# Chunk attention: dividing the output by turned reciprocals of the row sums, and ScalarE's copies ahead of its exponentials

## The chip, the cores and the metric

The kernel runs on one core of a Trainium2 chip, as one launch. The metric is the device time of that launch in microseconds (us). Each core has a matrix engine (TensorE, "PE" in the profile, its weight loads "PEld"), a vector engine (VectorE, "DVE"), a scalar engine (ScalarE, "ACT"), a general engine (GpSimd, "POOL") and a queue engine for transfers (SyncE, "SP"). Each works through its own list in order and waits on semaphores that the others raise.

## The reference

A two-layer encoder trunk over 512 positions of width 1024. Layer 0 mixes with a state-space model and a gated delta rule, layer 1 with chunk attention; both then have a cross-attention into 256 memory rows and a gated feed-forward block. Only layer 1's chunk attention is touched:

```python
def chunk_attention(h, w_qkv, w_out, q_g, k_g, rel_bias):   # CHUNK = 64, 16 heads of 64
    qkv = (h @ w_qkv).reshape(bsz, seq, 3, CA_HEADS, CA_HEAD_DIM)
    q = rms_norm(qkv[:, :, 0], q_g); k = rms_norm(qkv[:, :, 1], k_g); v = qkv[:, :, 2]
    # each chunk of 64 rows sees itself and the 8 chunks before it
        s = jnp.einsum('bqhd,bkhd->bhqk', q_c, k_c) * scale + bias
        s = jnp.where((band_pos + start) >= 0, s, -1e30)
        p = jax.nn.softmax(s, axis=-1)
        o = jnp.einsum('bhqk,bkhd->bqhd', p, v_c)
    return o @ w_out
```

## The kernel before

The program is written out by hand, engine by engine; nothing schedules it. Big products are done as three products of rounded parts (`product`, L325 to L327), the parts being made by ScalarE (`w_hi`, L293) and VectorE (`w_lo`, L297).

Chunk attention comes after its projection and the turning of q and k. It works on **pairs**: pair m (0 to 7) holds heads 2m and 2m+1, called e = 0 and 1. The 512 query rows are four tiles i of 128, and tile i sees i+1 tiles of keys, so its row of scores is 128, 256, 384 or 512 wide. Within a query tile the rows stand in reversed order, which the last step undoes.

For one pair the steps are:

- `ca_scores_pe` (L1951), TensorE: eight products of scores, tiles in the order 3, 2, 0, 1. Tile 1 goes into the bank that tile 3 had, so it waits until VectorE has taken tile 3's scores of both heads.
- `sums` (L2043), VectorE: adds the bias and takes each row's maximum, eight instructions; then the negated maxima (L2047).
- `exp` (L2015), ScalarE: eight exponentials, each with its row sums, read out by a short instruction behind it.
- `rescale` (L2057, L2061), VectorE: for each head one reciprocal of four columns of row sums, then four multiplications that divide the probabilities.
- `ca_turn_p_pe` (L1963), TensorE: 20 transposes in eight groups n (key tile s = n // 2, head e = n % 2) of 4, 4, 3, 3, 2, 2, 1 and 1. They use the three PSUM banks 4 to 6 in turn, so group n waits for the copy of group n-3.
- `ca_copy`: the eight groups are copied to SBUF, n = 0, 2, 5, 7 by ScalarE (L1989), n = 1, 3, 4, 6 by VectorE (L1991).
- `ca_values_pe` (L1973), TensorE: eight products of values and turned probabilities into bank 7, 64 partitions for each head. It waits until the pair before has left bank 7 (`c_ol`).
- L2032, ScalarE, rounds the outputs from bank 7 to `c_o_hi`; `out_lo` (L2051), VectorE, makes the rest `c_o_lo` from bank 7. When the last pair's rest is there, the output projection begins (L325 to L327).

The order across pairs: TensorE does turn(m), scores(m+2), values(m). ScalarE does the exponentials of pair m+1 with the copies of pair m strewn between them, then `c_o_hi` of pair m. VectorE does `out_lo`(m-1), the copies of pair m with `rescale`(m+1, head 0) among them, `sums`(m+2), `rescale`(m+1, head 1). GpSimd masks the bias rows and SyncE loads them; both are ahead by a pair.

Of the kernel before, what the change touches and what calls it, by code (L numbers as in the profile page):

```python
# [7 lines left out]
F32 = mybir.dt.float32  # L8
# [67 lines left out]
def build_program(nc, A):  # L76
    ctx = ExitStack()
    with ctx:
# [9 lines left out]
        with nc.sbuf_tensor("params", [P, N_PAR], F32) as par:  # L88
# [23 lines left out]
                   "c_pv2": ("sv_u", LEVELS * TT),  # L112
# [1752 lines left out]
            return ps[:, bank + e, c0:c0 + (i + 1) * P]  # L1865

        c_oT = (rounded("c_o_hi", arena, KT, SEQ), rounded("c_o_lo", at_b, KT, SEQ))


        def ca_proj_pe(pe):  # L1870
# [83 lines left out]
        def ca_turn_p_pe(pe, m):  # L1954
            for n in range(8):
                s, e = n // 2, n % 2
                g = 8 * m + n
                if g >= 3:
                    pe.wait_ge(sem(COPY[(g - 3) % 8][0]), 4 * ((g - 3) // 8) + COPY[(g - 3) % 8][1])
                for i in range(s, TT):  # L1960
                    if s == 0:
                        pe.wait_ge(sem(RESCALE[i][0]), after(RESCALE[i][0], RESCALE[i][1] * (2 * m + e) + RESCALE[i][2]))
                    ins = pe.transpose(ps[:, 4 + g % 3, i * P:(i + 1) * P], p_c(m, e, i)[:, s * P:(s + 1) * P], ident)  # L1963
                ins.then_inc(sem("c_tr"), 1)

        def ca_values_pe(pe, m):
            if m > 0:
                pe.wait_ge(sem("c_ol"), m)
            for s in range(TT):
                for e in range(2):  # L1970
                    pe.wait_ge(sem(COPY[2 * s + e][0]), 4 * m + COPY[2 * s + e][1])
# [7 lines left out]
        RESCALE = [("c_pv2", 4, 4), ("c_pv2", 4, 3), ("c_pv2", 4, 2), ("c_pv2", 4, 1)]  # L1979

        def ca_copy(eng, m, n):
            s, e = n // 2, n % 2
            g = 8 * m + n
            eng.wait_ge(sem("c_tr"), g + 1)
            if m >= 1:
                eng.wait_ge(sem("c_o"), m)
            dst, src = pT_c(e, s), ps[:, 4 + g % 3, s * P:SEQ]
# [24 lines left out]
        def ca_act(a):  # L2012
            def exp(m, e, i):
                p = p_c(m, e, i)
                a.activation(p, p, ACT.Exp, bias=c_neg[:, m % 2, e, i:i + 1], accum_out=c_sum[:, m % 2, e, i:i + 1]).then_inc(sem("c_exp"), 1)  # L2015

            a.wait_ge(sem("c_max"), 1)
            for e in range(2):
                for i in CA_EXP:
                    exp(0, e, i)  # L2020
            for m in range(CH // 2):
                if m + 1 < CH // 2:
                    a.wait_ge(sem("c_max"), m + 2)
                for e in range(2):
                    for j in range(4):
                        if m + 1 < CH // 2:
                            exp(m + 1, e, CA_EXP[j])
                        n = 4 * e + j
                        if COPY[n][0] == "c_pa":
                            ca_copy(a, m, n)  # L2030
                a.wait_ge(sem("c_o"), m + 1)
                a.activation(c_oT[0][:, m, :].rearrange("p (i n) -> p i n", i=TT),  # L2032
                                  ps[:, 7, :].rearrange("p (i n) -> p i n", i=TT)[:, :, ::-1], ACT.Copy).then_inc(sem("c_oc"), 1)

        def ca_dve(v):
            def sums(m):
                v.wait_ge(sem("c_mask"), after("c_mask", 2 * m + 2))
                if m >= 2:
                    v.wait_ge(sem("c_tr"), 8 * (m - 1))
                for n, i in enumerate(CA_ROWS):  # L2040
                    v.wait_ge(sem("c_s"), 4 * m + (1, 3, 3, 4)[n])
                    for e in range(2):
                        v.tensor_tensor_reduce(out=p_c(m, e, i), in0=ca_score(i, e),  # L2043
                                                    in1=bias_ring[:, (2 * m + e) % 4, BAND_W - (i + 1) * P:BAND_W], scale=1.0, scalar=-3.0e38,
                                                    op0=ALU.add, op1=ALU.max, accum_out=c_max[:, m % 2, e, i:i + 1]).then_inc(sem("c_s2"), 1)
                v.wait_ge(sem("c_s2"), 8 * m + 8)
                v.tensor_scalar(c_neg[:, m % 2], c_max[:, m % 2], -1.0, None, ALU.mult).then_inc(sem("c_max"), 1)  # L2047

            def out_lo(m):
                v.wait_ge(sem("c_oc"), m + 1)  # L2050
                v.tensor_tensor(c_oT[1][:, m, :].rearrange("p (i n) -> p i n", i=TT),  # L2051
                                ps[:, 7, :].rearrange("p (i n) -> p i n", i=TT)[:, :, ::-1],
                                c_oT[0][:, m, :].bitcast(F32).rearrange("p (i n) -> p i n", i=TT), ALU.subtract).then_inc(sem("c_ol"), 1)

            def rescale(m, e):
                v.wait_ge(sem("c_exp"), 8 * m + 4 * e + 4)
                v.reciprocal(c_rec[:, m % 2, e], c_sum[:, m % 2, e]).then_inc(sem("c_rec"), 1)  # L2057
                v.wait_ge(sem("c_rec"), after("c_rec", 2 * m + e + 1))
                for i in (3, 2, 1, 0):
                    p = p_c(m, e, i)  # L2060
                    v.tensor_scalar(p, p, c_rec[:, m % 2, e, i:i + 1], None, ALU.mult).then_inc(sem("c_pv2"), 1)  # L2061

            sums(0)
            sums(1)
            rescale(0, 0)
            rescale(0, 1)
# [12 lines left out]
            out_lo(CH // 2 - 1)  # L2079

        def ca_pool(g):
# [397 lines left out]
```

## Time and profile before

| | |
|---|---|
| median of 3 runs | 1754.69 us (1753.34 to 1756.93) |
| the profiled execution, its own time | 1754.25 us |
| its span in the trace | 1752.5 us |
| granted TensorE clock, mean | 0.988 of full |
| TensorE busy | 1654.1 us (94%) |
| VectorE, ScalarE, GpSimd busy | 777.7, 623.0, 218.2 us |
| chunk attention, first score to the output projection's first product | about 1061.8 to 1149.8 us of the span |

The page of the profile divides the span into busy time by engine, shows a chain of waits that ended last (86% TensorE, 8% VectorE, 3% ScalarE) and lists groups of instructions. Most of the span is TensorE's big products at full rate; a change elsewhere matters only where TensorE stands waiting. "Idle before" is what an engine lost ahead of an instruction, and "issue" is time in which it waited for nothing that the profile shows.

### The profile page before, as it was taken

How to read it: one execution, taken by the hardware profiler on the slowest of the kernel's cores; microseconds unless marked ns; L12 is line 12 of the kernel's file. 1: busy time of each engine (PE TensorE's matmuls, PEld its weight loads, DVE VectorE, ACT ScalarE, POOL GpSimd, SP SyncE). 2: the span in 40 equal slices, each digit the busy share in tenths (PEclk: the TensorE clock that was granted, in tenths of full speed). 3: DMA queues.
4: the chain of work that ended last, by engine and by line, in shares of the span. 5: the costliest groups of instructions: out<-in, count | busy, mean ns of one | idle time of the engine just before them, and what ended most of it. 6: DMA issues, size and time to landing. Idle time of an engine off the chain costs nothing.

```text
span 1752.5 us, 22603 instructions
## 1 busy us (share of the span) xinstructions
PE 1654.1 (94%) x9358; PEld 1349.4 (77%) x9358; DVE 777.7 (44%) x1011; ACT 623.0 (36%) x1006; POOL 218.2 (12%) x305
## 2 busy tenths in 40 slices
PE   5989989999989999999999997899998999999999
PEld 5778788777768788888888885478776878888887
DVE  4576435544444444442235437834343444444222
ACT  6443333344433322221124335634442432222110
POOL 3843034010000211110000000000000021111000
PEclk9999999999999999999999998999999999999999
DMA  6610112134103333332222331214311233333221
GB/s 204 125 49 11 62 51 74 49 111 144 58 24 96 96 96 96 96 96 96 96 96 89 99 101 37 85 49 144 121 48 49 72 96 96 96 96 96 96 96 72
DMA packets 146802, 151.85 MB, mean 87 GB/s; under 512 B 8865, under 2 KB 109345, under 8 KB 146593
## 3 DMA queue, kind: packets, MB, share of 16 engines
q1 hardware_dynamic: 146720, 150.69, 27.9%
q8 instruction: 60, 0.98, 0.2%
q14 instruction: 22, 0.17, 0.0%
HBM read 147.53 MB, written 3.15 MB: 86 GB/s over the span
## 4 chain that ended last, share of the span: by engine, by line
PE 86%; DVE 8%; ACT 3%; issue 2%; DMA 0%; SPq 0%; POOL 0%; DVEq 0%; ACTq 0%
PE ps L325 24%; PE ps L326 24%; PE ps L327 24%; PE ps L1639 2%; PE ps L1616 2%; PE ps L1973 1%; ACT w_hi L293 1%; PE ps L955 1%; DVE sb L2043 1%; DVE sb L601 1%; DVE w_lo_ab L297 1%; PE ps L1233 1%; PE ps L417 1%; ACT sb L2015 1%; PE ps L1244 1%
## 5 line engine op out<-in xcount | busy, mean ns | idle before, releaser
L325 PE MATMUL ps<-h_hi,w_hi 128*128 128x512 f32 x864 | 338.8, 392 | 3.9 <-DVE w_lo L1787 3.9
L326 PE MATMUL ps<-h_lo,w_hi 128*128 128x512 f32 x864 | 337.6, 391 | 0.0
L297 DVE TENSOR_TENSOR w_lo<-raw,w_hi 128x2048 fp32r<-128x2048 f32 x70 | 160.4, 2292 | 395.8 <-ACT w_hi L293 395.8
L293 ACT ACTIVATE w_hi<-raw 128x2048 fp32r<-128x2048 f32 x84 | 160.7, 1914 | 433.3 <-PE ps L327 432.6
L327 PE MATMUL ps<-h_hi,w_lo 128*128 128x512 f32 x704 | 274.5, 390 | 0.0
L325 PEld LDWEIGHTS ps<-h_hi,w_hi 128*128 128x128 f32 x864 | 162.9, 189 | 38.4 <-issue 4.7
L326 PEld LDWEIGHTS ps<-h_lo,w_hi 128*128 128x128 f32 x864 | 163.1, 189 | 33.5
L1787 DVE TENSOR_TENSOR w_lo<-raw,w_hi 128x2048 fp32r<-128x2048 f32 x44 | 138.1, 3138 | 53.5 <-ACT w_hi L1769 53.5
L327 PEld LDWEIGHTS ps<-h_hi,w_lo 128*128 128x128 f32 x704 | 132.6, 188 | 27.8
L1769 ACT ACTIVATE w_hi<-raw 128x2048 fp32r<-128x2048 f32 x44 | 84.3, 1916 | 161.1 <-PE ps L327 161.1
L325 PE MATMUL ps<-w_hi,a_hi 128*128 128x512 f32 x352 | 137.3, 390 | 1.7 <-DVE up L1785 1.7
L327 PE MATMUL ps<-w_hi,a_lo 128*128 128x512 f32 x352 | 137.0, 389 | 0.0
L326 PE MATMUL ps<-w_lo,a_hi 128*128 128x512 f32 x352 | 136.9, 389 | 0.0
L1797 POOL CAST a_hi<-up 128x512 f32 x44 | 27.0, 614 | 843.1 <-DVE up L1785 843.1
L325 PE MATMUL ps<-w_hi,h_hi 128*128 128x512 f32 x320 | 124.7, 390 | 2.3 <-DVE h_lo L430 2.3
L327 PE MATMUL ps<-w_hi,h_lo 128*128 128x512 f32 x320 | 124.5, 389 | 0.0
L326 PE MATMUL ps<-w_lo,h_hi 128*128 128x512 f32 x320 | 124.5, 389 | 0.0
L1785 DVE TENSOR_TENSOR up<-up,ps 128x512 f32<-128x512 f32 x44 | 30.2, 687 | 192.7 <-PE ps L327 188.9
L1765 ACT ACTIVATE up<-up 128x512 f32<-128x512 f32 x44 | 27.8, 632 | 153.4 <-DVE up L1781 153.3
L325 PEld LDWEIGHTS ps<-w_hi,a_hi 128*128 128x128 f32 x352 | 66.1, 188 | 16.1 <-DVE up L1785 2.5
L327 PEld LDWEIGHTS ps<-w_hi,a_lo 128*128 128x128 f32 x352 | 66.1, 188 | 13.8
L326 PEld LDWEIGHTS ps<-w_lo,a_hi 128*128 128x128 f32 x352 | 66.1, 188 | 13.6
(370 smaller groups left out, 2663.0 us busy)
## 6 DMA issues: line engine op xcount, KB each, us to landing
raw<-in_f_w_gate SPq DMA_DIRECT2D x44, 512.0 KB, 4.0
raw<-in_f_w_up SPq DMA_DIRECT2D x44, 512.0 KB, 5.3
raw<-in_f_w_down SPq DMA_DIRECT2D x44, 512.0 KB, 4.1
raw<-in_xa_w_kv SPq DMA_DIRECT2D x16, 1024.0 KB, 5.0
raw<-in_c_w_qkv SPq DMA_DIRECT2D x12, 1024.0 KB, 5.0
raw<-in_ab_w_in SPq DMA_DIRECT2D x10, 1024.0 KB, 5.9
raw<-in_xa_w_q SPq DMA_DIRECT2D x8, 1024.0 KB, 5.2
raw<-in_xa_w_out SPq DMA_DIRECT2D x8, 1024.0 KB, 5.0
```

The lines of the kernel that those rows point to most:

```text
L293: a.activation(w_hi[:, n % 2, :], raw[n % 2], ACT.Copy).then_inc(sem("w_hi"), 1)
L297: v.tensor_tensor(w_lo(n)[:, n % 2, :], raw[n % 2], w_hi[:, n % 2, :].bitcast(F32), ALU.subtract).then_inc(sem("w_lo"), 1)
L325: pe.matmul(out, a[0], b[0], start=start, stop=False)
L326: pe.matmul(out, a[0], b[1], start=False, stop=False)
L327: return pe.matmul(out, a[1], b[0], start=False, stop=stop)
L1616: ins = pe.matmul(ps[:, 2 * (h % 2) + i // 2, (i % 2) * 256:(i % 2) * 256 + 256], qT[:, 2 * h + d, i * P:(i + 1) * P], xk_T[:, 2 * h + d, ...
L1639: ins = pe.matmul(ps[:, 6 + d, :], xv[:, s, h * XD + d * P:h * XD + (d + 1) * P], pT_x[h % 2][:, s, :], start=(s == 0), stop=(s == 1))
L1765: a.activation(gsil[:, s, :], gsil[:, s, :], ACT.Silu).then_inc(sem(f"f{l}_silu"), 1)
L1769: a.activation(w_hi[:, slot, :], raw[slot], ACT.Copy).then_inc(sem("w_hi"), 1)
L1785: v.tensor_tensor(prod[:, s, :], gsil[:, s, :], ps[:, 2 * s + 1, :], ALU.mult).then_inc(sem(f"f{l}_free"), 1)
L1787: v.tensor_tensor(w_lo(n0)[:, slot, :], raw[slot], w_hi[:, slot, :].bitcast(F32), ALU.subtract).then_inc(sem("w_lo"), 1)
L1797: g.tensor_copy(aT[0][:, at], prod[:, s, :]).then_inc(sem(f"f{l}_ahi"), 1)
```

## The change

Four things are changed in chunk attention, and nothing elsewhere (one work buffer `c_rbc` of two times 512 columns is added).

1. `rescale` is gone: the probabilities are turned undivided, and the transposes wait for the exponentials themselves. VectorE takes the reciprocals of a pair in one instruction (`reciprocals`).
2. TensorE gets a ninth group in each pair: eight products that have a column of reciprocals, spread over 64 columns, as weights and the identity as the moving side. They lay each query's reciprocal along the 64 partitions of its head, in bank 6. ScalarE copies that to SBUF (`c_rb`).
3. The outputs are divided at the end: VectorE multiplies bank 7 by the turned reciprocals (`out_scaled`, `c_om`), ScalarE rounds that (`out_hi`), VectorE takes the rest (`out_lo`), now from SBUF. Values(m) waits for `c_om` of the pair before. `out_hi`(m-1) and `out_lo`(m-1) stand behind the copies of pair m.
4. ScalarE does its four copies of pair m first, then the reciprocals' copy and `out_hi`(m-1), and the eight exponentials of pair m+1 behind them.

```diff
@@ ca_turn_p_pe, TensorE, pair m @@
             for n in range(8):
                 s, e = n // 2, n % 2
...
+                bank_copied(pe, m, n)
                 for i in range(s, TT):
                     if s == 0:
-                        pe.wait_ge(sem(RESCALE[i][0]), after(RESCALE[i][0], RESCALE[i][1] * (2 * m + e) + RESCALE[i][2]))
-                    ins = pe.transpose(ps[:, 4 + g % 3, i * P:(i + 1) * P], p_c(m, e, i)[:, s * P:(s + 1) * P], ident)
+                        pe.wait_ge(sem("c_exp"), 8 * m + 4 * e + CA_EXP.index(i) + 1)
+                    ins = pe.transpose(ps[:, 4 + n % 3, i * P:(i + 1) * P], p_c(m, e, i)[:, s * P:(s + 1) * P], ident)
                 ins.then_inc(sem("c_tr"), 1)
+            bank_copied(pe, m, 8)
+            pe.wait_ge(sem("c_rec"), after("c_rec", m + 1))
+            for i in range(TT):
+                for e in range(2):
+                    ins = pe.matmul(ps[64 * e:64 * e + 64, 6, i * P:(i + 1) * P], c_rec[:, m % 2, e, i:i + 1].broadcast_to([P, CD]), ident,
+                                    start=True, stop=True)
+            ins.then_inc(sem("c_tr"), 1)
 
         def ca_values_pe(pe, m):
             if m > 0:
-                pe.wait_ge(sem("c_ol"), m)
+                pe.wait_ge(sem("c_om"), after("c_om", m))
...
+        def bank_copied(pe, m, n):
+            m, n = (m, n - 3) if n >= 3 else (m - 1, n + 6)
+            if m >= 0 and n < 8:
+                pe.wait_ge(sem(COPY[n][0]), 4 * m + COPY[n][1])
+            elif m >= 0:
+                pe.wait_ge(sem("c_rb"), after("c_rb", m + 1))
@@ ca_act, ScalarE @@
+            def out_hi(m):
+                a.wait_ge(sem("c_om"), after("c_om", m + 1))
+                a.activation(c_oT[0][:, m, :], c_rbc(m), ACT.Copy).then_inc(sem("c_oc"), 1)
...
             for m in range(CH // 2):
+                for n in range(8):
+                    if COPY[n][0] == "c_pa":
+                        ca_copy(a, m, n)
+                a.wait_ge(sem("c_tr"), 9 * m + 9)
+                if m >= 2:
+                    a.wait_ge(sem("c_ol"), m - 1)
+                a.activation(tiles(c_rbc(m)), tiles(ps[:, 6, :])[:, :, ::-1], ACT.Copy).then_inc(sem("c_rb"), 1)
+                if m > 0:
+                    out_hi(m - 1)
                 if m + 1 < CH // 2:
                     a.wait_ge(sem("c_max"), m + 2)
-                for e in range(2):
-                    for j in range(4):
-                        if m + 1 < CH // 2:
-                            exp(m + 1, e, CA_EXP[j])
-                        n = 4 * e + j
-                        if COPY[n][0] == "c_pa":
-                            ca_copy(a, m, n)
-                a.wait_ge(sem("c_o"), m + 1)
-                a.activation(c_oT[0][:, m, :].rearrange("p (i n) -> p i n", i=TT),
-                                  ps[:, 7, :].rearrange("p (i n) -> p i n", i=TT)[:, :, ::-1], ACT.Copy).then_inc(sem("c_oc"), 1)
+                    for e in range(2):
+                        for i in CA_EXP:
+                            exp(m + 1, e, i)
+            out_hi(CH // 2 - 1)
@@ ca_dve, VectorE @@
+            def out_scaled(m):
+                v.wait_ge(sem("c_o"), m + 1)
+                v.wait_ge(sem("c_rb"), after("c_rb", m + 1))
+                v.tensor_tensor(tiles(c_rbc(m)), tiles(ps[:, 7, :])[:, :, ::-1], tiles(c_rbc(m)), ALU.mult).then_inc(sem("c_om"), 1)
+
             def out_lo(m):
                 v.wait_ge(sem("c_oc"), m + 1)
...
+                v.tensor_tensor(c_oT[1][:, m, :], c_rbc(m), c_oT[0][:, m, :].bitcast(F32), ALU.subtract).then_inc(sem("c_ol"), 1)
+
+            def reciprocals(m):
+                v.wait_ge(sem("c_exp"), 8 * m + 8)
+                v.reciprocal(c_rec[:, m % 2], c_sum[:, m % 2]).then_inc(sem("c_rec"), 1)
...
             for m in range(CH // 2):
                 if m > 0:
-                    out_lo(m - 1)
+                    out_scaled(m - 1)
                 for n in range(8):
                     if COPY[n][0] == "c_pv":
                         ca_copy(v, m, n)
-                    if n == 4 and m + 1 < CH // 2:
-                        rescale(m + 1, 0)
+                if m > 0:
+                    out_lo(m - 1)
                 if m + 2 < CH // 2:
                     sums(m + 2)
                 if m + 1 < CH // 2:
-                    rescale(m + 1, 1)
+                    reciprocals(m + 1)
+            out_scaled(CH // 2 - 1)
             out_lo(CH // 2 - 1)
```

ScalarE, one pair in the middle of the stage. L2015 (before) and L2033 (after) are the exponentials, L1989 and L2007 the copies of turned probabilities. Before:

```order
L2032 ACTIVATE c_o_hi<-ps 128x512
L2015 ACTIVATE sb<-sb 128x512
L1989 ACTIVATE sb<-ps 128x512
L2015 ACTIVATE sb<-sb 128x384
L2015 ACTIVATE sb<-sb 128x256
L1989 ACTIVATE sb<-ps 128x384
L2015 ACTIVATE sb<-sb 128x128
L2015 ACTIVATE sb<-sb 128x512
L2015 ACTIVATE sb<-sb 128x384
L1989 ACTIVATE sb<-ps 128x256
L2015 ACTIVATE sb<-sb 128x256
L2015 ACTIVATE sb<-sb 128x128
```

And after:

```order
L2007 ACTIVATE sb<-ps 128x512
L2007 ACTIVATE sb<-ps 128x384
L2007 ACTIVATE sb<-ps 128x256
L2007 ACTIVATE sb<-ps 128x128
L2050 ACTIVATE c_rbc<-ps 128x512
L2037 ACTIVATE c_o_hi<-c_rbc 128x512
L2033 ACTIVATE sb<-sb 128x512
L2033 ACTIVATE sb<-sb 128x384
L2033 ACTIVATE sb<-sb 128x256
L2033 ACTIVATE sb<-sb 128x128
L2033 ACTIVATE sb<-sb 128x512
```

The copies have moved together to the front, one more copy from PSUM (L2050) stands behind them, and the rounding of the pair before now precedes the first exponential.

TensorE, one pair in the middle of the stage. L1963 and L1969 are the transposes, L1951 and L1959 the scores, L1973 and L1986 the values. Before:

```order
L1963 MATMUL ps<-sb 128x128 x20
L1951 MATMUL ps<-sb 128x512 x2
L1951 MATMUL ps<-sb 128x384 x2
L1951 MATMUL ps<-sb 128x128 x2
L1951 MATMUL ps<-sb 128x256 x2
L1973 MATMUL ps<-sb 64x512 x2
```

And after:

```order
L1969 MATMUL ps<-sb 128x128 x20
L1975 MATMUL ps<-sb 64x128 x8
L1959 MATMUL ps<-sb 128x512 x2
L1959 MATMUL ps<-sb 128x384 x2
L1959 MATMUL ps<-sb 128x128 x2
L1959 MATMUL ps<-sb 128x256 x2
L1986 MATMUL ps<-sb 64x512 x2
```

The eight products of reciprocals (L1975) stand between the transposes and the scores; nothing else moved there.

VectorE, between the negated maxima of one pair (L2047, now L2072) and the first sum of the next (named ISA here). Before:

```order
L2047 TENSOR_SCALAR sb<-sb 128x8
L2057 RECIPROCAL sb<-sb 128x4
L2061 TENSOR_SCALAR sb<-sb 128x512
L2061 TENSOR_SCALAR sb<-sb 128x384
L2061 TENSOR_SCALAR sb<-sb 128x256
L2061 TENSOR_SCALAR sb<-sb 128x128
L2051 TENSOR_TENSOR c_o_lo<-ps,c_o_hi 128x512
L1991 COPY sb<-ps 128x512
L1991 COPY sb<-ps 128x384
L1991 COPY sb<-ps 128x256
L2057 RECIPROCAL sb<-sb 128x4
L2061 TENSOR_SCALAR sb<-sb 128x512
```

And after:

```order
L2072 TENSOR_SCALAR sb<-sb 128x8
L2085 RECIPROCAL sb<-sb 128x8
L2077 TENSOR_TENSOR c_rbc<-ps,c_rbc 128x512
L2009 COPY sb<-ps 128x512
L2009 COPY sb<-ps 128x384
L2009 COPY sb<-ps 128x256
L2009 COPY sb<-ps 128x128
L2081 TENSOR_TENSOR c_o_lo<-c_rbc,c_o_hi 128x512
L2068 ISA sb<-ps,sb 128x512
```

The eight multiplications of a pair are gone, one 512-wide multiplication of the outputs has come, and `c_o_lo` has moved from ahead of the copies to behind them, directly ahead of the sums.

## Rows read from the trace of the kernel before

**Rows 1.** Busy time by engine in stretches, then TensorE's granted clock, DMA share, GB/s.

```profile
1096.00:1105.00 9.00, 7.22 (x50) 4.26 (x48) 8.10 (x29) 6.23 (x21) 0.29 (x2) 1.00 0.20 60
```

**Rows 2.** Chain of waits, first pairs and one later period: start, length (us), what.

```profile
1072.18 2.17 DVE sb L2043 x12
1074.37 0.17 DVE sb L2047
...
1077.38 3.85 PE ps L1963 x16
...
1087.28 0.03 ACT c_o_hi L2032
...
1106.62 0.03 ACT c_o_hi L2032
...
1110.28 0.19 DVE sb L2057
...
1111.89 1.31 DVE sb L2043 x4
...
1113.24 0.70 PE ps L1951 x4
1113.94 2.33 PE ps L1973 x16
1116.29 0.03 ACT c_o_hi L2032
...
1135.67 0.03 ACT c_o_hi L2032
```

**Rows 3.** Timeline of TensorE, one period: start, length, line, shapes, idle before.

```profile
1110.51 2.00 PE L1951 MATMUL ps<-sb 64*128 64x512 f32 x12
...
1116.17 0.66 PE L1963 MATMUL ps<-sb 128*128 128x128 f32 x4
```

**Rows 4.** Timeline of TensorE, the last pair, with no exponentials beside it.

```profile
1143.41 2.70 PE L1963 MATMUL ps<-sb 128*128 128x128 f32 x16 [0.43 <-DVE sb L2061]
1146.04 2.37 PE L1973 MATMUL ps<-sb 128*64 128x512 f32 x16
1149.84 0.50 PE L325 MATMUL ps<-w_hi,c_o_hi 128*128 128x512 f32 x1 [1.42 <-DVE c_o_lo L2051]
```

**Rows 5.** Timeline of PEld: eight loads of 128 columns (L1747), then a 64-column pair.

```profile
572.92 1.08 PEld L1747 LDWEIGHTS ps<-sb 128*128 128x128 f32 x8
573.92 0.19 PEld L325 LDWEIGHTS ps<-h_hi,w_hi 128*128 128x128 f32 x1
...
1096.52 0.14 PEld L1973 LDWEIGHTS ps<-sb 128*64 128x64 f32 x2
```

**Rows 6.** Timeline of ScalarE: eight exponentials in a row, then the last two c_o_hi.

```profile
1068.79 0.72 ACT L2015 ACTIVATE sb<-sb 128x512 f32<-128x512 f32 x1 [4.55 <-DVE sb L2047]
...
1073.07 0.19 ACT L2015 ACTIVATION_READ_ACCUMULATOR sb<-sb 128x1 f32 x1
...
1142.43 0.60 ACT L2032 ACTIVATE c_o_hi<-ps 128x512 fp32r<-128x512 f32 x1 [0.52 <-PE ps L1973]
1143.02 0.60 ACT L1989 ACTIVATE sb<-ps 128x512 f32<-128x512 f32 x1
...
1148.46 0.60 ACT L2032 ACTIVATE c_o_hi<-ps 128x512 fp32r<-128x512 f32 x1 [2.04 <-PE ps L1973]
```

**Rows 7.** Timeline of VectorE: the rest of a pair's outputs.

```profile
1097.58 0.69 DVE L2051 TENSOR_TENSOR c_o_lo<-ps,c_o_hi 128x512 fp32r<-128x512 f32 x1
```

**Rows 8.** Stretches of 2 us at the stage's start, columns as in Rows 1.

```profile
1064.00:1066.00 2.00, 0.00 (x0) 0.00 (x0) 2.00 (x4) 0.24 (x1) 0.00 (x0) 1.00 0.00 0
...
1068.00:1070.00 2.00, 1.40 (x4) 0.84 (x6) 0.72 (x5) 1.21 (x3) 0.00 (x0) 0.58 0.04 17
...
1074.00:1076.00 2.00, 0.01 (x1) 0.02 (x1) 1.93 (x9) 0.82 (x2) 0.00 (x0) 0.79 0.26 49
1076.00:1078.00 2.00, 1.72 (x7) 1.32 (x8) 1.29 (x5) 0.86 (x2) 0.15 (x1) 0.50 0.71 213
```

More of the change, by code:

```diff
@@ L111, in build_program @@
                    "f_gate": ("sv_y", LEVELS * TT), "f_rmm": ("r_kw", 2 * NCH), "f_rbc": ("r_om", NCH), "eps_rows": ("sv_d", LEVELS * TT),
-                   "c_pv2": ("sv_u", LEVELS * TT),
+                   "c_rb": ("sv_u", LEVELS * TT), "c_om": ("sv_t", (LEVELS - 1) * TT),
                    "c_mask": ("sv_mask", LEVELS * TT), "c_rec": ("sv_yc", LEVELS * TT),
@@ L1867, in build_program, with c_rbc, tiles @@
         c_oT = (rounded("c_o_hi", arena, KT, SEQ), rounded("c_o_lo", at_b, KT, SEQ))
+        c_rbc2 = tensor_at("c_rbc", at_f + 2056, F32, 2, SEQ)
+        def c_rbc(m):
+            return c_rbc2[:, m % 2, :]
+        def tiles(o):
+            return o.rearrange("p (i n) -> p i n", i=TT)
         def ca_proj_pe(pe):
@@ L1956, in ca_turn_p_pe @@
                 s, e = n // 2, n % 2
-                g = 8 * m + n
-                if g >= 3:
-                    pe.wait_ge(sem(COPY[(g - 3) % 8][0]), 4 * ((g - 3) // 8) + COPY[(g - 3) % 8][1])
+                bank_copied(pe, m, n)
                 for i in range(s, TT):
                     if s == 0:
-                        pe.wait_ge(sem(RESCALE[i][0]), after(RESCALE[i][0], RESCALE[i][1] * (2 * m + e) + RESCALE[i][2]))
-                    ins = pe.transpose(ps[:, 4 + g % 3, i * P:(i + 1) * P], p_c(m, e, i)[:, s * P:(s + 1) * P], ident)
+                        pe.wait_ge(sem("c_exp"), 8 * m + 4 * e + CA_EXP.index(i) + 1)
+                    ins = pe.transpose(ps[:, 4 + n % 3, i * P:(i + 1) * P], p_c(m, e, i)[:, s * P:(s + 1) * P], ident)
                 ins.then_inc(sem("c_tr"), 1)
+            bank_copied(pe, m, 8)
[5 more added lines that the diff above has]
+            ins.then_inc(sem("c_tr"), 1)
         def ca_values_pe(pe, m):
             if m > 0:
-                pe.wait_ge(sem("c_ol"), m)
+                pe.wait_ge(sem("c_om"), after("c_om", m))
             for s in range(TT):
@@ L1978, in build_program @@
         COPY = [("c_pa", 1), ("c_pv", 1), ("c_pa", 2), ("c_pv", 2), ("c_pv", 3), ("c_pa", 3), ("c_pv", 4), ("c_pa", 4)]
-        RESCALE = [("c_pv2", 4, 4), ("c_pv2", 4, 3), ("c_pv2", 4, 2), ("c_pv2", 4, 1)]
+        def bank_copied(pe, m, n):
[4 more added lines that the diff above has]
+                pe.wait_ge(sem("c_rb"), after("c_rb", m + 1))
         def ca_copy(eng, m, n):
             s, e = n // 2, n % 2
-            g = 8 * m + n
-            eng.wait_ge(sem("c_tr"), g + 1)
+            eng.wait_ge(sem("c_tr"), 9 * m + n + 1)
             if m >= 1:
                 eng.wait_ge(sem("c_o"), m)
-            dst, src = pT_c(e, s), ps[:, 4 + g % 3, s * P:SEQ]
+            dst, src = pT_c(e, s), ps[:, 4 + n % 3, s * P:SEQ]
             if COPY[n][0] == "c_pa":
@@ L2038, in sums @@
                 if m >= 2:
-                    v.wait_ge(sem("c_tr"), 8 * (m - 1))
+                    v.wait_ge(sem("c_tr"), 9 * (m - 1))
                 for n, i in enumerate(CA_ROWS):
@@ L2047, in sums @@
                 v.tensor_scalar(c_neg[:, m % 2], c_max[:, m % 2], -1.0, None, ALU.mult).then_inc(sem("c_max"), 1)
+            def out_scaled(m):
+                v.wait_ge(sem("c_o"), m + 1)
+                v.wait_ge(sem("c_rb"), after("c_rb", m + 1))
+                v.tensor_tensor(tiles(c_rbc(m)), tiles(ps[:, 7, :])[:, :, ::-1], tiles(c_rbc(m)), ALU.mult).then_inc(sem("c_om"), 1)
             def out_lo(m):
                 v.wait_ge(sem("c_oc"), m + 1)
[L2051 to L2061, printed above, removed]
+                v.tensor_tensor(c_oT[1][:, m, :], c_rbc(m), c_oT[0][:, m, :].bitcast(F32), ALU.subtract).then_inc(sem("c_ol"), 1)
+            def reciprocals(m):
+                v.wait_ge(sem("c_exp"), 8 * m + 8)
+                v.reciprocal(c_rec[:, m % 2], c_sum[:, m % 2]).then_inc(sem("c_rec"), 1)
             sums(0)
             sums(1)
-            rescale(0, 0)
-            rescale(0, 1)
+            reciprocals(0)
             for m in range(CH // 2):
                 if m > 0:
-                    out_lo(m - 1)
+                    out_scaled(m - 1)
                 for n in range(8):
```

## The prediction, made before the changed kernel had run

> **What bounds the kernel now.** I read the busy shares first, then the stretches, then the chain of waits inside chunk attention, then each engine's timeline there. Over the span TensorE is busy 94%, so only a place where it stands waiting can pay. Chunk attention is such a place: in nine microseconds of its middle TensorE is busy 7.22, VectorE 8.10 and ScalarE 6.23 [rows 1]. No engine is full, so the stage runs by a loop of waits, and the reader is to look for that loop. From the rounding of pair 0's output at 1087.28 to that of pair 5 at 1135.67 there are five periods in 48.39 us, 9.68 us each [rows 2]. One period, from 1106.62: ScalarE rounds, then does exponentials and copies by turns until the first head's row sums are ready (3.66 us, to 1110.28); VectorE's reciprocal, four divisions and a copy (1.61, to 1111.89); its first two sums (1.35 with the hand-over, to 1113.24); TensorE's last two scores (0.70); the values (2.33). That is 9.67 [rows 2]. VectorE's work on the probabilities and ScalarE's interleaving are on this loop; the first scores of a pair are not [rows 3].
>
> **The change, part by part.** The path of the new period is read from the lists: values(m-1) end, 20 transposes of pair m, the eight new products, ScalarE's copy of the reciprocals, `out_hi`(m-1), VectorE's `out_lo`(m-1), two sums, TensorE's last scores, values(m). The rounding that closed a pair now stands between TensorE's new products and the sums that TensorE waits for. Priced:
>
> - Transposes with the copies in between and no exponentials in the way: the last pair of before shows groups 1 to 7 and their copies, 1143.41 to the values at 1146.04, 2.63 us [rows 4]. The first group of four adds about 0.5 of the 0.66 of its row (the rest is the drain of its last), and it starts 0.12 before the values end (1116.17 against 1116.29) [rows 2, 3]. The copy of the last group needs no waiting for now, 0.1 off. About 2.9 us. `out_scaled` of the pair before (0.69, as its like [rows 7]) lies on VectorE ahead of its first copy, and is done while TensorE turns groups 0 and 1.
> - Eight products with 64-column weights over 128 columns. The trace has none by themselves. Upper bound: four products with 128-column weights take 1.00 us to issue (loads from 572.92 to 573.92) [rows 5], 2.0 for eight. Lower bound: the values of 128 columns. Their two products begin at 1096.52 [rows 5], and sixteen records of the values, 5120 columns in two passes, take 2.33 us [rows 2], so 256 columns (128 in two passes) take 0.11 to 0.12; eight make 0.9. I take 0.9, since these rows have the same weights' width and the same halves of partitions; 0.2 for the drain of the last. Together 1.1. The two rows differ in their loads: 1.08 us for eight of 128 columns, 0.14 for a pair of 64 [rows 5]. The Trainium skill ("TensorE: Matmul & The Clock Gate", Part 2, step on LDWEIGHTS) says that the time of a weight load scales with its column count and not with its rows; by it the new loads are half as long as those of the upper bound, and the sum would stay at the lower one.
> - The reciprocals' copy: the next ScalarE instruction starts 0.5 to 0.6 after one of 512 columns (1142.43 to 1143.02) [rows 6], then `out_hi` 0.60, with hand-overs about 1.2.
> - `out_lo`: 0.69 [rows 7], the next may start 0.6 after it. Two sums and the hand-over 1.35 [rows 2]. Together 1.95. Its source moves from PSUM to SBUF; no row shows the second kind, so I keep the 0.69 and hold 0.1 either way for possible.
> - Last scores and values 0.70 + 2.33 = 3.03 [rows 2].
>
> Sum 2.9 + 1.1 + 1.2 + 1.95 + 3.0 = 10.15, so **0.48 more in each period**. There are five (pairs 1 to 5, those which both close a pair before and have scores of pair m+2 in front of their values): +2.4. The exponentials of the next pair lie beside that: eight take 4.47 us (1068.79 to 1073.26) [rows 6], and from the end of `out_hi` there are 1.95 + 3.03 us to the next transposes, so they are covered by half a microsecond.
>
> The ends of the stage are priced singly.
>
> - Start. The divisions of pair 0 go. Before, sums(1) end at 1074.37, the transposes that count run 1077.38 to 1081.23 and the first values end at 1087.28 [rows 2]. Now transposes can start at once after the second scores; VectorE still does sums(1) until 1074.5 before its first copy. From there: copies and transposes to 1076.6, the new products 1.1, the scores 2.0 [rows 3] with the two sums beside their second half, last scores and values 3.03, and 0.5 of waits: about 1083.3 at full clock, 4 earlier. A part of this stretch ran at half clock before (0.58 at 1068, 0.50 at 1076) [rows 8]; if it does so again the new products, scores and values take some 3 us more, 1 earlier in all. I take 3 earlier: -3.0.
> - Pair 6 has no scores in front of its values. Before, 1135.67 to 1142.43, 6.76 us [rows 2, 6]; after, turning 2.9, products 0.9, values 2.4: 6.2. -0.5.
> - Pair 7. Before, 1142.43 to 1148.46, 6.03 us [rows 6]: its exponentials had run between the copies of pair 6. Now all eight start after pair 6's reciprocals are copied and `out_hi`(5) is done. The products of pair 6 end 2.2 before its values do. Then 1.1 of ScalarE and 4.5 of exponentials: 3.4 us after the values' end. Then 2.5 of transposes of groups 1 to 7, 0.9 of products, 2.4 of values: 9.2. +3.15. Here the cover is gone that the exponentials had.
> - Tail. Before, 1148.46 to 1149.84, 1.38 us [rows 4, 6]; now `out_scaled`, `out_hi`, `out_lo` in a row, 0.69 + 0.60 + 0.69 and hand-overs, 2.1. +0.7.
> - TensorE now stands for most of 3.4 us before pair 7, and for 2.1 in the tail. At the stage's start such a gap was followed by half clock (no product at 1064 to 1066, 0.58 at 1068; none at 1074 to 1076, 0.50 at 1076) [rows 8]. I put +0.7 for it, between nothing and the 3.5 that half clock through pair 7 would cost.
> - Waits on two semaphores that were one (new products, bank 7's successors): +0.1 in each of 8 pairs, +0.8. Its bounds are 0 and 0.2 each.
>
> Sum: +2.4 - 3.0 - 0.5 + 3.15 + 0.7 + 0.7 + 0.8 = +4.25. Made against the profiled execution's own 1754.25 us (0.44 below the median of the runs shown), that gives **1758.5 us**. VectorE's relief, eight divisions a pair, is real, but it is spent in waiting. The transfers of the bias rows and GpSimd's masks hang on sums that are a pair back, and nothing is queued behind them that matters here.
>
> **Rivals.**
>
> *The new products run at the pace of the 128-column loads.* Then 2.0 for 0.9 in all 8 pairs, +9: 1767.5. For it: weights that are one column spread out stand in the one row with that pace. Against it: those loads are twice as wide [rows 5].
>
> *Half clock through pair 7 and through the start.* For it: what rows 8 show after each gap, and a gap of 3.4 us that was not there. Then +3.5 instead of +0.7 at the end, and -1 instead of -3 at the start: 1763.3. The Trainium skill ("TensorE: Matmul & The Clock Gate", Part 1) says that the low clock is the default and activity lifts it, so a long gap is paid for behind the gap; the trace agrees for the two gaps at the start, and by that rule alone this rival would be the forecast.
>
> *The period stays as it is.* The transposes, free of the exponentials, might need 2.4 rather than 2.9, since in rows 4 VectorE's first copy was late by `out_lo`. Then the periods cost nothing, the last pair 2.7, and the start gives its 3: 1755.5, no change.
>
> *Faster: the busiest engine set the period.* If the stage in truth followed VectorE (8.10 of 9, 8.7 of a period [rows 1]), taking about 2 us off it in each period leaves TensorE as the fullest: 7.22 of 9 is 7.8 a period, and 0.9 of products makes 8.7. One microsecond off in five periods, the start's 3 and 0.5, against 3.15 and 0.7 at the end: -4.7, 1749.5. It decides if `out_hi` and `out_lo` get through before TensorE has done its first scores; by the order of the lists they come 3.1 us after the new products, and the first scores take 2.0 [rows 3], so I give it little.
>
> **How the numbers follow.** Forecast 0.40 (its own range 1756 to 1761.5), 128-column pace 0.14, half clock 0.20, period unchanged 0.19, faster 0.07. A measurement of this kernel can tell 0.2%, 3.5 us, from no change: slower begins at 1758.2. The forecast lies just over it and gives half its chance, 0.22 to slower and 0.18 to same; with the two costly cases slower is 0.56, same 0.36 with the unchanged period, faster 0.08. The range 1753.5 to 1766 leaves out the faster case and the worst of the 128-column pace.
>
> **What the changed profile would show.** The distance between two ends of the values in the middle: 10.15 us against 9.68 (8.7 for the faster rival, over 11 for the 128-column pace). In the chain of waits: `c_rbc`, `c_o_hi` and `c_o_lo` between the new products and the sums, and no exponentials there. The sixteen records of the new products within 1.1 us. The first values end at 1083 to 1086. The gap on TensorE before pair 7 of about 3.4 us, and the granted clock behind it. The forecast is wrong if the exponentials are in the middle's chain, or if the stage ends before 1149.84.

## The result and the profile after

The changed kernel takes 1757.97 us (median of 20 runs, 1754.20 to 1762.17); the kernel before took 1754.74 in 20 runs beside it (1752.78 to 1756.93). The ratio is 1.0018, 95% interval 1.0011 to 1.0024: slower by 3.2 us, clear of noise but a little under the 0.2% that the prediction called its bound. The forecast was 1758.5.

Outside the stage, profiled executions differ among themselves by more than the change costs. The first sum of pair 0 starts at 1065.18 before and 1067.41 after, behind the same instructions, and over the fourteen profiles of this text that start moves between 1063.76 and 1069.06, and the time behind the stage between 599.5 and 602.9. (The last section says what goes with this.) So I compare **the stage's length**, from the first sum to the output projection's first product: 84.66 before, 88.86 after, +4.20. The chain of waits after, one period and the two ends of it (start, length, what):

```profile
1106.36 2.46 PE ps L1969 x18
1108.83 0.01 issue
1108.83 0.33 PE ps L1969
1109.16 0.00 issue
1109.17 0.33 PE ps L1969
1109.49 1.05 PE ps L1975 x16
1110.54 0.02 issue
1110.56 0.60 ACT c_rbc L2050
1111.16 0.53 ACT c_o_hi L2037
1111.69 0.02 issue
1111.71 0.06 DVE c_o_lo L2081
1111.77 0.55 issue
1112.32 1.32 DVE sb L2068 x4
1113.63 0.04 issue
1113.68 0.70 PE ps L1959 x4
1114.38 2.31 PE ps L1986 x16
1116.69 2.46 PE ps L1969 x18
```

The reader is to see three things. The exponentials are gone from it; before, these stood in the same chain between the rounding at 1106.62 and the reciprocal at 1110.28 of [rows 2], with copies and "issue" between them:

```profile
1107.12 0.11 ACT sb L2015
...
1107.73 0.19 ACT sb L2015
...
1108.81 0.68 ACT sb L2015 x3
...
1109.87 0.39 ACT sb L2015 x2
```

TensorE's new products (L1975), ScalarE's two copies and VectorE's `c_o_lo` stand in a row in front of the sums. And the period, 1106.36 to 1116.69, is 10.33 us against 9.68. VectorE had been relieved as intended:

```profile
1105.00:1114.00 9.00, 7.75 (x65) 5.03 (x62) 5.60 (x17) 5.89 (x19) 0.29 (x2) 1.00 0.19 58
```

Its busy time in nine microseconds (third number behind the length) is 5.60 where it was 8.10 [rows 1]; the relief went into waiting for `c_o_hi`, 2.2 us in every period. VectorE's timeline of the changed kernel:

```profile
1111.71 0.69 DVE L2081 TENSOR_TENSOR c_o_lo<-c_rbc,c_o_hi 128x512 fp32r<-128x512 f32 x1 [2.22 <-ACT c_o_hi L2037]
```

TensorE's timeline at the stage's end, which answers to [rows 4]:

```profile
1141.32 2.32 PE L1986 MATMUL ps<-sb 128*64 128x512 f32 x16
1144.97 0.63 PE L1969 MATMUL ps<-sb 128*128 128x128 f32 x4 [1.33 <-ACT sb L2033]
1147.15 3.68 PE L1969 MATMUL ps<-sb 128*128 128x128 f32 x16 [1.55 <-ACT sb L2033]
1150.84 1.09 PE L1975 MATMUL ps<-sb 128*64 128x128 f32 x16
1151.76 2.32 PE L1986 MATMUL ps<-sb 128*64 128x512 f32 x16
1156.27 0.50 PE L325 MATMUL ps<-w_hi,c_o_hi 128*128 128x512 f32 x1 [2.18 <-DVE c_o_lo L2081]
```

Pair 7 waits for its exponentials (L2033) twice, and its sixteen transposes take 3.68 us where they took 2.70 [rows 4]. The granted clock of these stretches (the third number from the end) is the reason: 0.50 is TensorE's lower level, 1.2 GHz, and 1.00 its upper one, 2.4 GHz. It falls behind TensorE's waits of 1.33 and 1.55 us, and again behind the tail:

```profile
1146.00:1148.00 2.00, 0.85 (x4) 0.88 (x5) 0.77 (x2) 1.49 (x7) 0.00 (x0) 0.78 0.00 0
1148.00:1150.00 2.00, 2.00 (x12) 1.97 (x10) 1.14 (x2) 0.49 (x1) 0.00 (x0) 0.50 0.00 0
...
1158.00:1160.00 2.00, 2.00 (x6) 1.53 (x5) 1.62 (x1) 0.00 (x0) 0.00 (x0) 0.50 0.00 0
```

### The profile page after: what moved, and what is told of

It is laid out like the page before. It is cut to its first block, busy times and chain, and to the rows that moved or that the text cites. A ratio compares the mean times of both kernels' runs of the same rounds, so it can differ in the third digit from the quotient of the medians.

```text
span 1757.5 us, 22825 instructions
## 1 busy us (share of the span) xinstructions
PE 1663.5 (95%) x9486; PEld 1356.5 (77%) x9486; DVE 763.1 (43%) x947; ACT 630.2 (36%) x1014; POOL 218.3 (12%) x305
## 3 DMA queue, kind: packets, MB, share of 16 engines
HBM read 147.53 MB, written 3.15 MB: 86 GB/s over the span
## 4 chain that ended last, share of the span: by engine, by line
PE 86%; DVE 8%; ACT 3%; issue 2%; DMA 0%; SPq 0%; POOL 0%; DVEq 0%; ACTq 0%
PE ps L325 24%; PE ps L326 23%; PE ps L327 23%; PE ps L1616 2%; PE ps L1639 2%; PE ps L1969 1%; ACT w_hi L293 1%; PE ps L1986 1%; PE ps L955 1%; DVE sb L2068 1%; DVE sb L601 1%; DVE w_lo_ab L297 1%; PE ps L1233 1%; PE ps L417 1%; PE ps L1244 1%
```

## The experiments

Periods are the mean distance between the ends of the values of pairs 0 and 5, the stage is as above, both from one profile each. Ratios are to the kernel before, run beside it on the same chip; medians of different rows come from different chips. "Half clock" below is a granted clock of 0.5. It stands in pair 7 of the changed kernel, e1, e3, e4 and e9, and in pair 6 of e6 and e10.

| kernel | period | pair 6, pair 7 | stage | median us | ratio, 95% interval |
|---|---|---|---|---|---|
| before | 9.68 | 6.78, 6.01 | 84.66 | 1754.74 | |
| changed | 10.32 | 6.30, 10.44 | 88.86 | 1757.97 | 1.0018 (1.0011 to 1.0024) |
| e1 products twice | 11.20 | 7.18, 11.23 | 95.44 | 1762.95 | 1.0047 (1.0031 to 1.0063) |
| e2 old ScalarE order | 12.23 | 7.93, 6.31 | 100.39 | 1766.25 | 1.0066 (1.0049 to 1.0083) |
| e3 new order alone | 13.49 | 8.00, 7.59 | 109.03 | 1776.80 | 1.0127 (1.0111 to 1.0144) |
| e4 sums first | 9.78 | 6.30, 11.60 | 87.25 | 1755.93 | 1.0003 (0.9994 to 1.0012) |
| e5 idle work | 10.33 | 6.31, 9.38 | 87.58 | 1757.13 | 1.0020 (1.0010 to 1.0030) |
| e6 sums first, pair 7 covered | 9.77 | 9.48, 6.30 | 84.76 | 1754.29 | 1.0005 (0.9996 to 1.0014) |
| e7 sums first, idle work | 9.77 | 6.32, 9.37 | 84.67 | 1754.22 | 1.0003 (0.9994 to 1.0012) |
| e8 e6, copies by turns | 9.69 | 7.58, 6.23 | 82.58 | 1748.16 | 0.9972 (0.9961 to 0.9984) |
| e9 changed, copies by turns | 10.24 | 6.23, 10.32 | 88.21 | 1757.21 | 1.0011 (1.0002 to 1.0020) |
| e10 changed, pair 7 covered | 10.32 | 9.63, 6.31 | 87.90 | 1756.45 | 1.0011 (1.0002 to 1.0020) |
| e11 e8, products in the gap | 10.51 | 7.60, 6.23 | 87.44 | 1755.82 | 1.0012 (1.0002 to 1.0023) |
| e12 e11, one wait freed | 9.05 | 7.97, 6.23 | 78.97 | 1744.83 | 0.9962 (0.9946 to 0.9979) |

**e1: the new products twice.**

```diff
+            for again in range(2):
+              for i in range(TT):
                 for e in range(2):
```

> The changed kernel with the eight new products of every pair issued twice (the same values again). Loop theory (a period is: transposes, new products, reciprocals' copy, out_hi, out_lo, two sums, last scores, values; 10.33 us in the changed kernel's profile): sixteen more records take 0.85 us, the sixteen of now are on that path, so the period goes to about 11.2, pairs 0, 6 and 7 pay as well, and the time goes to about 1765 (+7). Rival, the new products are beside the work that counts (ScalarE's and VectorE's own lists set the period): period 10.3, time 1758.

Its chain of waits:

```profile
1096.94 1.92 PE ps L1976 x32
1098.87 0.02 issue
1098.89 0.60 ACT c_rbc L2051
1099.49 0.53 ACT c_o_hi L2038
```

32 records take 1.92 where 16 took 1.05, so sixteen cost 0.87 and the drain the remaining 0.18. The period grows by the same 0.88 to 11.20: all sixteen are on the path. The time rose by 5 us to 1762.95 where the stage rose by 6.6.

**e2: the turned reciprocals with ScalarE's old order.**

```diff
+                if m + 1 < CH // 2:
+                    a.wait_ge(sem("c_max"), m + 2)
                 for n in range(8):
+                    if m + 1 < CH // 2:
+                        exp(m + 1, n // 4, CA_EXP[n % 4])
                     if COPY[n][0] == "c_pa":
                         ca_copy(a, m, n)
                 a.wait_ge(sem("c_tr"), 9 * m + 9)
...
-                    for e in range(2):
-                        for i in CA_EXP:
-                            exp(m + 1, e, i)
```

> The changed kernel with ScalarE's old order: the exponentials of pair m+1 strewn between the copies of pair m, then the reciprocals' copy and out_hi. Loop theory: each copy comes later by the exponentials ahead of it, so turning takes longer and all that hangs on it; period about 12 (10.33 now), but pair 7 gets back to about 6 us (10.5 now) since its exponentials are covered; in all about +5, 1763. Rival, the cover of pair 7 and the ends are what costs, and the order in the middle does nothing: period 10.3, time 1754.

Period 12.23, pair 7 back at 6.31. Both halves are as the loop theory had them; three of the five periods are 11.95 and the other two, which hold half clock, 12.4 and 12.9. The time is 3 us above the expected 1763. The change's first three parts alone cost more than three times what the whole does.

**e3: ScalarE's new order in the kernel before.**

```diff
-                for e in range(2):
-                    for j in range(4):
-                        if m + 1 < CH // 2:
-                            exp(m + 1, e, CA_EXP[j])
-                        n = 4 * e + j
-                        if COPY[n][0] == "c_pa":
-                            ca_copy(a, m, n)
+                for n in range(8):
+                    if COPY[n][0] == "c_pa":
+                        ca_copy(a, m, n)
+                if m + 1 < CH // 2:
+                    a.wait_ge(sem("c_max"), m + 2)
+                    for e in range(2):
+                        for i in CA_EXP:
+                            exp(m + 1, e, i)
```

> The kernel before with only ScalarE's order changed: all four copies of a pair first, the eight exponentials of the next pair then, divisions as before. Loop theory: the divisions of the next pair's first head stand on VectorE ahead of the last copy and of the sums, and now wait for exponentials that begin only after the copies; about 3.0 + 2.2 + 1.7 + 0.2 + 1.35 + 0.7 + 2.3, period 11.5 (9.68 before), and pair 7 uncovered too: time 1765 to 1768. Rival, the order by itself is the gain and the turned reciprocals the loss: period under 9.7, time at or below 1754.

```profile
1120.77 2.18 ACT sb L2015 x8
...
1123.59 0.87 DVE sb L2060 x3
...
1124.66 1.23 DVE sb L2042 x4
...
1125.93 0.70 PE ps L1951 x4
1126.64 4.02 PE ps L1973 x16
```

The exponentials, divisions, sums, scores and values stand in one row, as expected. My 11.5 for the period was too low; it is 13.49. The values take 4.02 rather than 2.33, and not by waiting: TensorE is busy without a pause, at a granted clock of 0.57 over these four microseconds.

```profile
1126.60:1130.60 4.00, 4.00 (x19) 1.57 (x17) 2.87 (x16) 0.00 (x0) 0.00 (x0) 0.57 0.29 81
```

In this order TensorE stands 3.55 us before its last scores, and half clock follows in each of the five periods; that is 1.7 of the 13.49, and the loop at full clock would be about 11.8. Pair 7 took 7.59 for 6.01, about 1.0 of it half clock again. So neither half of the change is good by itself: they need each other.

**e4: VectorE's sums ahead of `out_lo`.**

```diff
-                if m > 0:
-                    out_lo(m - 1)
                 if m + 2 < CH // 2:
                     sums(m + 2)
+                if m > 0:
+                    out_lo(m - 1)
```

> The changed kernel with VectorE's sums(m+2) ahead of out_lo(m-1). Loop theory: the reciprocals' copy, out_hi and out_lo (2.2 us of waiting on VectorE) leave TensorE's path; what is next is ScalarE's loop: reciprocals' copy, out_hi, eight exponentials (5.5 us), groups 1 to 7 and the new products (3.6): period 9.2 to 9.5; with five such periods 5 us less than the changed kernel, 1753. Rival, TensorE is the bound already (busy 9 of 10.3 with the new products): period 10.0 or more, time 1757.

Period 9.78, between the two theories. ScalarE is off the chain, but its loop is not what is next; TensorE's is: transposes, products, first scores, 0.69 of waiting for the two sums, last scores, values.

```profile
1112.96 0.70 PE L1959 MATMUL ps<-sb 64*128 64x256 f32 x4 [0.69 <-DVE sb L2068]
```

I had left the first scores' 1.3 us out, up to where VectorE may begin.

**e5: idle work in the gaps at the stage's end.**

```diff
+        def ca_warm_pe(pe, n):
+            for k in range(n):
+                pe.matmul(ps[:, 0, 0:P], ident, ident, start=True, stop=True)
...
+                if m == CH // 2 - 1 and n == 1:
+                    ca_warm_pe(pe, 5)
...
+                if m == CH // 2 - 2:
+                    pe.wait_ge(sem("c_s2"), 4 * CH)
+                    ca_warm_pe(pe, 4)
+                if m == CH // 2 - 1:
+                    ca_warm_pe(pe, 7)
```

> The changed kernel with idle TensorE work laid into the three gaps at the stage's end: four products of the identity with itself after values(6), five between the first and second group of pair 7, seven after values(7), all into an unused bank that nothing reads. Clock theory (TensorE's half clock after the gaps is part of the loss: pair 7's transposes took 3.68 us against 2.70 in the kernel before, and eight products of the output projection 0.43 against 0.23): the granted clock stays at 1.0 from 1140 on, 2.7 us less than the changed kernel, about 1755.3. Rival, the gaps cost only their own length: the clock changes or not, time 1758.

```profile
1144.00:1148.00 4.00, 3.33 (x27) 2.52 (x28) 2.69 (x6) 2.48 (x10) 0.00 (x0) 1.00 0.00 0
1152.00:1156.00 4.00, 3.57 (x20) 2.92 (x19) 2.39 (x2) 2.28 (x2) 0.00 (x0) 1.00 0.00 0
```

The clock stays whole there and pair 7 is 1.06 shorter, yet the time does not tell the kernel from the changed one (1.0020 and 1.0018). The two intervals leave room for a saving of some 1.8 us at most (an estimate from their widths), so the expected 2.7 is not there. In this profile half clock came instead at 1308, behind the stage, and the time behind the stage is the changed kernel's, 601.3 and 601.2. e7, below, has the same ratio as its twin too.

**e6: e4, and pair 7's exponentials between pair 6's copies.**

```diff
+                last = m == CH // 2 - 2
+                if last:
+                    a.wait_ge(sem("c_max"), m + 2)
                 for n in range(8):
+                    if last:
+                        exp(m + 1, n // 4, CA_EXP[n % 4])
                     if COPY[n][0] == "c_pa":
                         ca_copy(a, m, n)
...
-                if m + 1 < CH // 2:
+                if m + 1 < CH // 2 and not last:
```

> Sums ahead of out_lo as in the run before, and ScalarE's old order for pair 6 alone: pair 7's exponentials strewn between pair 6's copies. Cover theory (pair 7 is long because its exponentials lost their cover): pair 6 about 1.8 longer, pair 7 about 6.1 instead of 10 and more, the gap gone and the clock whole behind it; 3 us less than with the sums first alone, 1753. Rival, what pair 7 wins pair 6 loses: 1756, no change.

Pair 6 took 9.48 (3.2 more, not 1.8), pair 7 6.30. The cover theory had the exponentials' price right and the clock wrong: in this profile half clock stands in pair 6 itself, behind a wait of 1.29 us. The new products take 1.98 there and 1.09 in e8, and with the values half clock adds about 1.5.

```profile
1135.76 1.98 PE L1975 MATMUL ps<-sb 128*64 128x128 f32 x16 [1.29 <-ACT sb L2007]
```

```profile
1135.00:1139.00 4.00, 3.24 (x20) 2.24 (x22) 0.07 (x1) 2.86 (x10) 0.00 (x0) 0.57 0.00 0
```

Pairs 6 and 7 together take 15.8 against 17.9, the stage is 2.5 shorter; the ratios of the two, 1.0005 and 1.0003, do not separate them.

**e7: e4 with the idle work of e5.**

> Sums ahead of out_lo, and the same idle work in the gaps as in e5. If the two savings are independent: period 9.77, clock 1.0 behind the gaps, about 2.5 us less than with the sums first alone, 1753.4. If not, 1756.

Stage 84.67, 2.6 less than e4: the profile of e4 has half clock in pair 7 (0.58 in 1148 to 1152) and this one has none. The ratio is e4's, 1.0003. The profiled execution of e7 was the shortest of its eleven (1749.93, their median 1754.22), so its clock is not that of the others.

**e8: e6 with the copies by turns.**

```diff
-        COPY = [("c_pa", 1), ("c_pv", 1), ("c_pa", 2), ("c_pv", 2), ("c_pv", 3), ("c_pa", 3), ("c_pv", 4), ("c_pa", 4)]
+        COPY = [("c_pa", 1), ("c_pv", 1), ("c_pa", 2), ("c_pv", 2), ("c_pa", 3), ("c_pv", 3), ("c_pa", 4), ("c_pv", 4)]
```

> As e6, and the copies of turned probabilities taken strictly by turns (ScalarE n = 0, 2, 4, 6, VectorE 1, 3, 5, 7). With the sums first the period is TensorE's own chain with 3.1 us of turning, in which VectorE's four copies run back to back for 2.07 us and TensorE waits twice for them. If VectorE's share of the copies bounds turning: turning 2.8, period 9.45, 1.5 us less than e6, 1751.5. If the three banks bound it: period 9.77 as in e6.

In the middle this is worth 0.08 a period and not 0.3; that the three banks bound the turning fits, but no run changes them. Pair 6 is 1.9 shorter: about 0.3 of it by the copies and the rest because this profile has no half clock there.

```profile
1135.20 1.09 PE L1975 MATMUL ps<-sb 128*64 128x128 f32 x16
```

The time fell by more than the stage did (6 against 2.2). The profiled executions differ by 5.55, which is the 2.2 and 3.4 behind the stage, where e6's has half clock twice and e8's never. The mean granted clock of all executions says the same: 0.9875 in e6's eleven, 0.9911 in e8's seven.

**e9 and e10: those two edits in the changed kernel, each alone.**

> The changed kernel with the copies of turned probabilities taken strictly by turns and nothing else. If the alternation by itself is what made e8 fast (its period was 9.69 against 9.77 in e6, but its time 6 us lower): time about 1754. If it is worth 0.08 in a period and 1.9 in the interleaved pair 6 only: period about 10.25, time 1757.5.

> The changed kernel with pair 7's exponentials strewn between pair 6's copies and nothing else. Cover theory: pairs 6 and 7 together fall from 16.7 to about 15.8 as in e6 (9.5 and 6.3), the clock stays whole or nearly behind them, stage 88 us or less; time 1756. Rival: 1758, what pair 7 wins pair 6 loses.

e9 has a period of 10.24 and a time of 1757.21. e10 has pairs 6 and 7 at 15.9 together (16.7 in the changed kernel) and 1756.45; as in e6, its profile has half clock in pair 6 (0.57 over 1141 to 1145). Small gains, both as the second reading or the cover theory said; neither interval excludes the other's value or the changed kernel's. The alternation alone did not make e8 fast.

**e11 and e12: the products in TensorE's gap.** `ca_recs_pe` holds the new products, `ca_scores_pe` calls it ahead of the last scores, and ScalarE takes the reciprocals' copy and `out_hi` between the two heads' exponentials. Of the edit only the call is shown:

```diff
                 if n == 3:
+                    if m >= 2:
+                        ca_recs_pe(pe, m - 2)
                     pe.wait_ge(sem("c_s2"), 8 * m + 2)
```

> e8 with the eight new products moved into the wait that TensorE has before its last scores (0.69 us in e8), and the reciprocals' copy and out_hi on ScalarE moved between the two heads' exponentials. If the new products on TensorE's chain are now what is left: the gap hides 0.7 of their 0.9, period 8.9 to 9.1 (9.69 in e8), five periods, time 1745. Rival, ScalarE's loop (copies, eight exponentials, two copies, about 9.3 with the wait for the products) takes over: period 9.3 to 9.5, time 1747. Rival 2: c_om comes later and holds VectorE's copies up, period as in e8 or longer, 1748 and more.

It got slower than e8, period 10.51. VectorE's timeline of e11 names the cause:

```profile
1111.38 0.69 DVE L2081 CUSTOM_DVE_ANT_0 sb<-ps,sb 128x512 f32<-128x512 f32 x1 [2.76 <-PE ps L1979]
```

The first sum waited 2.76 us for the new products (L1979), not for the scores. The change had rewritten that wait from `8 * (m - 1)` to `9 * (m - 1)`, which counts the ninth group too; harmless where the products stand ahead of the scores. e12 asks for what the sums need:

```diff
-                    v.wait_ge(sem("c_tr"), 9 * (m - 1))
+                    v.wait_ge(sem("c_tr"), 9 * (m - 2) + 8)
```

> e11 with one number changed: sums(m) waits for the eight transposed groups of pair m-2 and no longer for its ninth group, the new products, too. In e11 VectorE's first sum began 0.1 us after the new products' end, 3.1 after the first scores' start, and the period was 10.5. Wait theory: that wait alone spoilt e11; the sums begin 1.3 after the scores' start, behind the products TensorE waits no more, period 8.9 to 9.3, stage about 80 us, time 1745 to 1747. Rival, ScalarE's later reciprocals' copy and out_hi are the bound: period stays near 10.5, time 1755.

VectorE's timeline and TensorE's share of e12:

```profile
1105.02 0.69 DVE L2081 CUSTOM_DVE_ANT_0 sb<-ps,sb 128x512 f32<-128x512 f32 x1 [0.92 <-PE ps L1961]
```

```profile
1099.00:1108.00 9.00, 8.81 (x70) 5.47 (x68) 6.76 (x25) 7.13 (x23) 0.29 (x2) 1.00 0.18 58
```

The sum now waits for the scores (L1961), 1.3 after they start; TensorE is busy 8.81 of 9, the period is 9.05. At 1744.83 this is the fastest version, 0.38% below the kernel before (0.9946 to 0.9979). Seven of its nine executions took 1743.9 to 1745.6 at a granted clock of 0.990 to 0.992, the other two 1752.9 and 1753.6 at 0.985. Between the profiles 8.7 us lie: 5.7 are the stage, and 3.1 lie behind it, where the kernel before has half clock twice and this one never.

## Why the prediction was right

The median came out 0.5 under the forecast, and the direction was right; the chances leaned to more than 0.2% slower (0.56), and the ratio of 1.0018 lies just inside the band called same (whose parts add up to 0.37, not 0.36, and leave 0.07 for faster). The closeness is in part luck: as a difference to the kernel before, +4.25 was forecast and +3.2 measured, and 0.5 of that gap is hidden by starting from one execution that lay under the median. In its steps:

- *What bounds the stage is a loop of waits, and VectorE's relief is spent in waiting.* Right: VectorE fell from 8.10 to 5.60 of 9 and the period rose; e4 shows that what stood in its place was `out_hi` and `out_lo`, for moving them off gave 0.55 a period.
- *The new path, 10.15.* It was 10.33, link by link: transposes 2.9, measured 3.13 (to 1109.49); products with drain 1.1, measured 1.05; reciprocals' copy and `out_hi` 1.2, measured 1.17; `out_lo`, two sums and hand-over 1.95, measured 1.97; last scores and values 3.03, measured 3.01. Only the transposes were mis-sized, by 0.2. Groups 1 to 7 took 2.64, as the 2.63 of [rows 4]; the 0.1 taken off for the last copy did not show, and the last two groups, of one transpose each, still wait for VectorE's copies (L2009), which stand back to back there (the two 0.33 in the chain). The rest is the head start over the values' end, 0.07 here, and the drain.
- *The new products at the pace of the values of 128 columns, not of the 128-column loads.* Right, shown by e1: 0.87 for sixteen records. The trace shows what makes them cheap: the records of the two heads, which write different halves of the partitions, start 0.007 us apart, and the next two 0.109 behind them, while L1747's start singly, 0.111 apart. The Trainium skill's rule on weight loads ("TensorE: Matmul & The Clock Gate", Part 2) pointed to the lower bound too, but the trace does not bear it out as the reason: loads of 137 ns for L1975 against 187 to 192 for L1747 are not half, and the 128-column loads of the transposes (L1969) take 141 ns in the median.
- *The start, -3.0.* The first values ended 22.06 after the first sum before and 18.31 after: -3.75. The forecast's 3 stood between its two cases, 4 at full clock and 1 at half, and was 0.75 too small: the clock was at half until about 1075 and whole behind it, so the new products, scores and values ran near the first case.
- *Pair 6, -0.5.* 6.78 to 6.30, right.
- *Pair 7, +3.15.* +4.43, of which 0.98 is the transposes at half clock, which had its own term; with the clock held (e5) pair 7 is 9.38, +3.4. e10 gives pair 7 its cover back and it falls to 6.31: the missing cover was the cause. That pair 6 pays most of it back (9.63 for 6.30, about 1.7 of it half clock) I had not priced, since the change does not do it.
- *Tail, +0.7.* 1.43 to 2.19, right.
- *Clock, +0.7.* In the profiled execution 1.0 in pair 7 and 1.7 behind the tail (eight products of the projection at 0.43 for 0.23, and a part of one). So the term was too small for this profile. For the medians its size is not shown: with both gaps filled (e5) the ratio was the same within 1.8 us.
- *Waits on two semaphores, +0.8.* Not found as such; 0.2 a period in the transposes is in their term above. Here errors cancelled: this term was 0.8 too large and the periods 0.8 too small, and the start's 0.75 went against pair 7's and the clock's.

Term by term for the profiles: periods +3.2 (forecast 2.4), start -3.75, pair 6 -0.5, pair 7 +4.4, tail +0.8: +4.2 for the stage. The two executions also differ by +2.2 ahead of the stage and -1.4 behind it, which the other profiles show to vary without the change.

Rivals: the 128-column pace is refuted by e1. Half clock came in part: 1.0 us in pair 7 and 1.7 behind the tail rather than 3.5, and at the start none behind 1075. The unchanged period is refuted in its mechanism (10.33), though its verdict, same, is what the ratio came to. The faster rival's condition, `out_hi` and `out_lo` off the path, did not hold; e4 made it hold, and the stage shrank.

What stays open is where half clock falls. The changed kernel's twenty executions spread over 8 us (six within 1754.2 to 1755.4) where those of before spread over 4, and their times go with the mean granted clock: the six shortest had 0.989 to 0.991, the three longest 0.985 to 0.986. In every kernel with seven executions or more the longer ones tend to have the lower clock. Why one execution gets more of it than another no run shows, and so the part of each median that is the schedule's own is known only through the stage's length.

## What to carry to other kernels

Write the loop of waits link by link from the rows before counting an engine's relief: work taken off an engine pays only if the step that replaces it does not stand between two engines that wait for each other, and `out_lo` was worth 0.55 us a period merely by standing behind the sums. Price the last round of a pipeline by itself, because work that was covered by the next round's loses its cover there. When steps are moved, read every counted wait again: one that counts a group too many is free in one order and cost 1.5 us a period in the next (e11 and e12).

## What the runs showed that I had not expected

Half clock is a real price, and where it falls differs from one execution to the next. Behind the stage all fourteen kernels do the same work, and the time there takes three values, by how often the granted clock falls to 0.5 in it:

| times at half clock behind the stage | profiles | time behind the stage |
|---|---|---|
| none | e1, e2, e3, e4, e7, e8, e12 | 599.5 to 599.6 |
| once | changed, e5, e9, e10, e11 | 601.2 to 601.3 |
| twice | before, e6 | 602.6 to 602.9 |

So each time cost 1.7 us. The kernel before and e7 in the same ten microseconds, TensorE busy 7.34 in both:

```profile
1300.00:1310.00 10.00, 7.34 (x32) 6.28 (x31) 4.62 (x6) 3.86 (x16) 0.00 (x0) 0.83 0.00 0
```

```profile
1300.00:1310.00 10.00, 7.34 (x33) 5.14 (x32) 5.91 (x8) 3.15 (x12) 0.00 (x0) 1.00 0.01 2
```

Half clock in one profile is therefore not yet a time that removing its gap gives back: with the clock held at 1.0 from 1144 to 1156, e5 and e7 had the ratios of their twins. Where the schedule brings it in every period, as in e3, it is 1.7 us each time. And a stage in the middle is measured better by its own length than by the whole: behind identical instructions its start moved by 5.3 us over fourteen profiles, more than the change, and the time behind it by 3.4.
